# A two-layer hybrid decoder step: convolution, FFN, embedding and attention stages token-major, with the residual in HBM

## The reference

```python
for i in range(2):                                     # layer 0 convolution + FFN, layer 1 attention + experts
    hn = rms_norm(h, norm_mix[i])
    if i == 0:
        a, gate = split(hn @ w_pw1 + b_pw1)
        u = a * sigmoid(gate)
        u_ext = concat([past, u])                      # past: zeros, or 30 rows of state for sample tokens
        c = depthwise_conv(u_ext, w_dw) + b_dw         # 31 taps, causal
        y = silu(layer_norm(c)) @ w_pw2 + b_pw2
    else:
        q = head_rms_norm(hn @ w_q)                    # 16 heads
        y = softmax_window_sink(q, k, v) @ w_o         # keys t-128..t, one learned sink logit per head
    h = h + y
    hn = rms_norm(h, norm_ffn[i])
    h = h + (swiglu(hn) if i == 0 else top2_of_8_expert_swiglu(hn))
    h = h + sigmoid(rms_norm(h, norm_ple[i]) @ ple_gate[i]) * (p[i] @ ple_proj[i])
    if i == 0:
        s = rms_norm(h, norm_kv)
        k, v = head_rms_norm(s @ w_k), s @ w_v         # shared K/V; sample tokens add 128 cached rows
```

## Time and profile before

| | us |
|---|---|
| median of 3 runs (4354.18 to 4480.99) | 4356.48 |
| profiled run | 4348.89 |
| its span, slowest core (4335.1 to 4347.6 over the cores) | 4347.6 |

### The profile page before, as it was taken

How to read it: one execution, slowest core, us unless ns; L and a number is a source line. 1 busy time by engine, 2 the same in 40 slices (tenths; PEclk the granted TensorE clock), 3 DMA queues, 4 the chain that set the end, 5 groups by cost and what they waited for, 6 DMA issues and landing times.

```text
span 4347.6 us, 48773 instructions; the slowest of 8 cores (4335.1 to 4347.6 us)
## 1 busy us (share of the span) xinstructions
PE 2992.9 (69%) x20283; PEld 1866.0 (43%) x20291; DVE 1687.9 (39%) x2406; ACT 996.3 (23%) x1936; POOL 666.7 (15%) x728
## 2 busy tenths in 40 slices
PE   0365756656899968654664160269999999999654
PEld 0322222222455523211112020159987798888511
DVE  0132221224566674788995022631211122111154
ACT  0033233331111123343553000111111122111111
POOL 0010101000000004001502511211111111111144
PEclk9986877767999978878676575579999999999877
DMA  7500000003223120011501529359989899998254
GB/s 160 136 5 0 0 0 0 0 2 50 38 32 43 20 44 10 1 17 7 13 1 4 11 36 173 119 118 166 162 152 157 130 169 179 174 174 148 69 133 113
DMA packets 434769, 322.62 MB, mean 74 GB/s; under 512 B 312750, under 2 KB 356830, under 8 KB 434444
## 3 DMA queue, kind: packets, MB, share of 16 engines
q0 software_dynamic: 364416, 231.82, 35.7%
q1 hardware_dynamic: 64844, 76.85, 6.5%
q10 hardware_dynamic: 5280, 10.75, 1.0%
HBM read 475.67 MB, written 53.14 MB: 122 GB/s over the span
## 4 chain that ended last, share of the span: by engine, by line
PE 54%; DVE 14%; DMA 7%; issue 7%; ACT 5%; POOL 4%; DVEq 0%; POOLq 0%; ACTq 0%; SPq 0%
PE pb L1065 23%; PE pb L544 18%; PE pb L572 9%; DVE arena L1702 3%; DVE arena L1071 3%; DMA arena<-ck 3%; DVE arena L1083 2%; ACT arena L1225 1%; POOL arena L817 1%; DMA XG<-arena 1%; DMA arena<-arena 1%; POOL arena L171 1%; DVE arena L1705 1%; POOL XG L171 1%; POOL arena L159 1%
## 5 line engine op out<-in xcount | busy, mean ns | idle before, releaser
L1065 PE MATMUL pb<-arena 128*128 128x512 bf16 (+4 forms) x6284 | 1340.1, 376 | 463.2 <-ACT arena L1075 141.4
L1065 PEld LDWEIGHTS pb<-arena 128*128 128x128 bf16 (+1 forms) x6284 | 608.6, 104 | 1193.1 <-issue 288.5
L544 PE MATMUL pb<-arena 128*128 128x0 bf16 x7168 | 795.0, 274 | 0.8 <-DVE arena L505 0.8
L544 PEld LDWEIGHTS pb<-arena 128*128 128x128 bf16 x7168 | 679.1, 98 | 113.4 <-issue 1.1
L552 DVE TENSOR_TENSOR arena<-arena,pb 128x640 bf16<-128x640 f32 x224 | 184.0, 821 | 653.4 <-PE pb L544 647.7
L572 PE MATMUL pb<-arena 128*128 128x0 bf16 x3584 | 404.5, 274 | 0.0
L572 PEld LDWEIGHTS pb<-arena 128*128 128x128 bf16 x3584 | 337.7, 98 | 54.5
L551 ACT ACTIVATE arena<-pb 128x640 f32<-128x640 f32 x224 | 157.7, 704 | 617.2 <-PE pb L544 617.2
L1071 DVE RECIPROCAL arena<-arena 128x512 f32<-128x512 f32 (+2 forms) x92 | 245.9, 2673 | 76.6 <-ACT arena L1070 76.6
L1361 DVE TENSOR_TENSOR arena<-arena,pb 128x413 f32<-128x413 f32 (+1 forms) x440 | 225.8, 578 | 0.0
L1702 DVE RECIPROCAL arena<-arena 128x512 f32<-128x512 f32 x64 | 214.6, 3353 | 18.8 <-ACT arena L1698 17.3
(11 more groups left out here) (211 smaller groups left out, 2319.7 us busy)
## 6 DMA issues: line engine op xcount, KB each, us to landing
arena<-moe_gu POOLq DMA_DIRECT2D x224, 512.0 KB, 7.8
arena<-moe_d POOLq DMA_DIRECT2D x128, 448.0 KB, 9.2
XG<-arena ACTq DMA_DIRECT2D x1, 10240.0 KB, 69.5
arena<-XG SPq DMA_DIRECT2D x8, 1280.0 KB, 33.2
YD<-arena SPq DMA_DIRECT2D x8, 1280.0 KB, 18.3
arena<-x SPq DMA_DIRECT2D x16, 512.0 KB, 4.0
h4D<-arena SPq DMA_DIRECT2D x16, 512.0 KB, 2.8
arena<-h4D SPq DMA_DIRECT2D x16, 512.0 KB, 5.0
```

Of the source, the lines that this page charges most:

```text
L544: last = e.matmul(bank(b + h, HALF).shape_from_register(sr), w[:, a, kc, :], xg[:, kc, h * HALF:(h + 1) * HALF].shape_from_register(sr), s ...
L1065: last = e.matmul(banks[bk][0:prow, 0:ncols], l, rr, start=(i == 0), stop=(i == len(pairs) - 1))
```

## The change

Everything ahead of `Tail.experts` is written anew, token-major, the tokens of a tile on the partitions. The experts and the final stage keep their code. What it does, stage by stage:

- Weights are packed on the host in the order in which they lie in SBUF. The residual lives in HBM between the stages (h1D, h3D, h4D, fp32); x is loaded in 17 tiles where tile t holds the rows 16b+t. The norm of a tile is a Square with accumulated sum on ACT, an added eps on DVE, a power of -1/2 on POOL and one multiply on DVE, then eight transposes on PE.
- pw1 stays feature-major over tiles of 413 tokens (`T5`). Chunks 0 and 1 are issued inside the x loop. The copies to ks, vs and convs are queued on SP behind the x loop and in front of the past-row loads. u goes to HBM (uD, bf16) and comes back with 8 channels x 16 token phases on the partitions; the convolution of a chunk is then 48 matmuls of 128 columns against a tap matrix that DVE builds (`tbuild`, 6144 elements), adding b_dw on DVE out of PSUM, token-major.
- LayerNorm by bn_stats on DVE, one Identity pass and eight SiLU passes on ACT per pair of tiles; pw2 token-major; x is reloaded and b_pw2 added to it on POOL; the sum is stored to h1D.
- FFN: the activations `hact` of all 22 blocks stay in SBUF in bf16. The down product accumulates over 22 blocks in PSUM for each token tile, in one loop with the embedding term. The zero fill of XG is issued at block 4 of gate/up.
- K/V and Q weights are loaded as fp32 and scaled by the norm's gain on ACT and DVE, in memory that `hact` held until then.
- K/V, Q, attention, Wo and routing are one loop of 22 iterations, each working on up to five tiles in different steps. V has a column of ones, which gives the denominator; the mask is a multiply on DVE by 0 or 1; the reciprocal is of 128x16. The sample caches are loaded on the POOL queue in iterations 1 to 4 into one buffer and used in iterations 2 to 5. `route_b` is split in `route_l` and `route_c`. Nine units of the expert ring are loaded before the loop, the other 18 after it.

```diff
@@ x loop, and what follows it
+    for t in range(NB):
+        cur = xnorm(t)
+        if pend is not None:
+            xturn(*pend)
+        pend = cur
+        if nxt < NB:
+            pre_x(nxt)
+            nxt += 1
+        while oi < len(order) and T5[order[oi][1]][0] + T5[order[oi][1]][1] <= t * 128 and oi < 2 * (t - 3):
+            pw1(*order[oi])
+            oi += 1
+    S.dma("sp", ks[:, 0:127, :], ck[:, 1:128, :], "d2d0")
+    S.dma("sp", vs[:, 0:127, :], cv[:, 1:128, :], "d2d1")
+    S.dma("sp", convs[:, 0:29, :], sc[:, 1:30, :], "d2d2")
+    past_parts()
+    for c in range(8):
+        uout(c)
+        ustate(c)
+        if c >= 1:
+            conv(c - 1)
+        if c + 1 < 8:
+            tbuild(c + 1)
+        if c + 2 < 8:
+            for g in range(5):
+                pw1(c + 2, g)
+    conv(7)
@@ u round trip and convolution of a chunk
+    def uout(c):
+        S.dma("pool", uD[c * 128:(c + 1) * 128, :], u[:, 0:SEQ], "uo%d" % (c % 2), r=[u_r], w=[uD_r[c]])
+        S.dma("sp", U[:, :, 2:130], uD[c * 128:(c + 1) * 128, :].rearrange("(g c) (t b) -> (c t) g b", c=8, t=16), ...)
+    def conv(c):
+        for q in range(4):
+                for g4 in range(4):
+                    for dl in range(3):
+                        last = e.matmul(bank(bk, 128, 128, g4 * 128), U[:, g, 2 - dl:130 - dl], T[:, g, dl * 128:(dl + 1) * 128], ...)
+            S.op("dve", lambda e: e.tensor_tensor(out=ct[...], in0=bank(bk)[...], in1=bdw[...], op=ALU.add), ...)
@@ pw2
+    def x2_load(t):
+        S.dma("sp", b[0:n, :], xph[t] if t < 16 else xs[:, :], sem, w=[r_])
+        S.op("pool", lambda e: e.tensor_tensor(out=b[0:n, :], in0=b[0:n, :], in1=b2[0:n, :], op=ALU.add), r=[b2_r], w=[r_])
@@ FFN down
+                for h_ in range(2):
+                    for f in range(k0, k1):
+                        lt = hact[:, f, n_ * 128:n_ * 128 + n]
+                        last = e.matmul(bank(bk + h_, 512, n), lt, Wd[:, f, h_ * 512:(h_ + 1) * 512], start=(f == 0), stop=(f == NF - 1))
@@ sample caches
+    def s_load(sg):
+        for si in range(4):
+            S.dma("pool", KA5[0:127, si, :, 0, :], ck[s_, 1:128, :]..., "ka%d" % si, w=[KA_r], part=(si > 0))
+            S.dma("pool", VA5[0:127, si, :, 0, :], cv[s_, 1:128, :]..., "va%d" % si, w=[VA_r], part=(si > 0))
+            S.dma("pool", V05[0:1, si, :, 0, :], cv[s_, 0:1, :]..., "v0%d" % si, w=[V0g_r], part=(si > 0))
@@ the attention loop
+    for i in range(17 + 5):
+        if on is not None:
+            ot = o_turn(*on)
+        if qk is not None:
+            qk_turn(*qk)
+        if i == 1:
+            s_load(0)
+        xt_ = x_turn(*xn_) if xn_ is not None else None
+        for g in range(4):
+            if na is not None:
+                scores(na, g)
+            if g == 0 and xt_ is not None:
+                lo_ = tl.route_l(*xt_, 6, 256)
+            if g == 1 and lo_ is not None:
+                tl.route_c(*lo_, 6, 256)
+            if np_ is not None:
+                pv(np_, g)
+            if g == 1 and ot is not None:
+                xn_ = oproj(*ot)
+        if np_ is not None:
+            on = onorm(np_)
+        if nq is not None:
+            qk = qkv(nq)
+        if 2 <= i < 6:
+            s_att(i - 2)
+            if i < 5:
+                s_load(i - 1)
+    tl.ring_open(PRE, tl.RING_N)
```

More of the change, by code:

```diff
@@ new lines, in s4_out @@
+    def s4_out(n_, n, xn, xn_r):
+        bk = nb()
+        turn(xn, xn_r, n, bk)
+        xT, xT_r = xT4.next()
+        copy("act", xT[:, :, 0:n], turned(bk, n), [b_r[bk]], [xT_r])
+        S.dma("sp", x3D[n_ * 128:(n_ + 1) * 128, :].rearrange("p (k c) -> p k c", k=8)[:, :, 0:n], xT[:, :, 0:n], "x3s%d" % ((n_ + 1) % 17 % 4), r=[xT_r], w=[x3D_r[n_]])
+    S.dma("sp", gp0, rows[7:8, :].to_broadcast([128, D]), "gp0", w=[gp0_r])
+    for i in range(2):
+        s4_load(order4[i])
+    q1 = q2 = None
@@ new lines, in build, with scores, fn @@
+    pgs = {}
+    def scores(n_, g):
+        qT, qT_r, kT, kT_r, _, _ = kvs[n_]
+        bs = pair()
+        k0 = 0 if n_ > 0 else 1
+        kt = {1: (kT, kT_r)}
+        if n_ > 0:
+            kt[0] = kvs[n_ - 1][2:4]
+        def fn(e):
+            last = None
+            for kb in range(k0, 2):
+                for hf in range(2):
+                    sl = slice(64 * hf, 64 * hf + 64)
+                    last = e.matmul(bank(bs + hf, 256, 128, kb * 256), kt[kb][0][sl, g, :], qT[sl, 2 * g:2 * g + 2, :], start=True, stop=True)
+            return last
+        S.op("pe", fn, r=[qT_r] + [v[1] for v in kt.values()], w=[b_r[bs], b_r[bs + 1]])
+        pb, pb_r = Pr.next()
+        src = P[:, bs * 512:(bs + 2) * 512].rearrange("p (h c) -> p h c", h=2)[:, :, k0 * 256:512]
+        dst = pb[:, :, k0 * 256:512]
+        S.op("act", lambda e: e.activation(out=dst, in_=src, func=AF.Exp), r=[b_r[bs], b_r[bs + 1]], w=[pb_r])
+        mk = maskt.rearrange("p k j q -> p (k j q)")[:, k0 * 256:512].unsqueeze(1).to_broadcast([128, 2, 512 - k0 * 256])
+        S.op("dve", lambda e: e.tensor_tensor(out=dst, in0=dst, in1=mk, op=ALU.mult), r=[c_mask], w=[pb_r])
+        pgs[(n_, g)] = (pb, pb_r)
@@ new lines, in o_turn, with oproj, fn @@
+    def o_turn(n_, ob, ob_r):
+        turn(ob, ob_r, 128, 6)
+        OT, OT_r = OTr.next()
+        copy("dve", OT, turned(6, 128), [b_r[6]], [OT_r])
+        return n_, OT, OT_r
+    def oproj(n_, OT, OT_r):
+        n = rowsof(n_)
+        bo = pair()
+        def fn(e):
+            last = None
+            for h in range(2):
+                for kc in range(8):
+                    last = e.matmul(bank(bo + h, 512, n), OT[:, kc, 0:n], Wo[:, kc, h * 512:(h + 1) * 512], start=(kc == 0), stop=(kc == 7))
+            return last
+        S.op("pe", fn, r=[OT_r, Wo_r], w=[b_r[bo], b_r[bo + 1]])
+        h, h_r = h5t.pop(n_)
+        S.op("dve", lambda e: e.tensor_tensor(out=h[0:n, :], in0=P[0:n, bo * 512:(bo + 2) * 512], in1=h[0:n, :], op=ALU.add),
+             r=[b_r[bo], b_r[bo + 1]], w=[h_r])
+        S.dma("sp", h4D[n_ * 128:n_ * 128 + n, :], h[0:n, :], "h4s%d" % (n_ % 4), r=[h_r], w=[tl.h4D_r[n_]])
+        ms, rs, ms_r, rs_r, _ = mcol(n)
+        xn, xn_r = xn5.next()
+        square(h[0:n, :], xn[0:n, :], ms, n, [h_r], ms_r, xn_r)
+        powh(ms, rs, ms_r, rs_r, n)
+        S.op("dve", lambda e: e.scalar_tensor_tensor(out=xn[0:n, :], in0=h[0:n, :], scalar=rs, in1=gf1[0:n, :], op0=ALU.mult, op1=ALU.mult),
+             r=[h_r, rs_r, gf1_r], w=[xn_r])
+        return n_, n, xn, xn_r
@@ L1732, in build, with s_first2, s_att @@
+    def s_first2():
+        turn(K0s, K0s_r, NS, 4, nk=4)
+        copy("dve", k0T, turned(4, NS, 4), [b_r[4]], [k0T_r])
+    def s_att(sg):
+        b0 = pair()
         for hb in range(2):
-            bk = nb()
             def fnt(e):
@@ L1795, in build @@
[L1795 to L1799 removed]
+                    e.matmul(bank(b2_, 4, 128, col), VA[:, si, g * 128:(g + 1) * 128], PA[:, col:col + 4], start=True, stop=False)
```

1795 lines of the change are left out of this document (838 added, 957 removed).

## The result

The changed kernel takes 3571.09 us (median of 4 runs, 3564.76 to 3643.28) against 4370.66 us of the kernel before on the same chip: ratio 0.8176 with a 95% interval of 0.8119 to 0.8233. Its profiled execution spans 3562.8 us; the prediction's sum was 3322 us, forecast 3325, range 3020 to 3515. The direction was right, the sum was short by 241 us, and the time lies above the upper end of the range. Some executions ran with one die at a lower granted clock; the ratios leave them out, where a run has no ratio its profiled execution stands for it, and f4_two_buffers is read on a core of the other die.

What follows compares the result with a forecast made beforehand. The prediction took the chain between engines to bound all changeable stages but the PE-full FFN. Its terms A to G summed to 3322 us; a few us more for the median gave the forecast 3325 us, range 3020 to 3515.

Steps and rivals of the forecast that it cites:

- F: K/V/Q, attention, Wo and routing in one loop: 661 us, loaded iterations 62 us each, full ones 27.5 us.
- C: LayerNorm, pw2 and norm: 222 us, 24 us a pair of tiles, with POOL's x reload and bias add in the chain.
- E: Wkv/Wq staging after the last down matmul: 50 us with PE idle, 42 us of it for 8 MB.
- D: FFN: gate/up 315 us, down with the embedding term 258 us, the zero fill lying beside gate/up.
- A: Load, norm, pw1 of two chunks and past rows: 158 us, all on the path.
- B: Convolution loop: 145 us, six chunks with pw1 at 20 us each, plus 25 us for the last two.
- G: Transition to the experts 36 us, as ring units compete with gathered rows; experts and final stay at 1477 us.
- R3: Rival, expert ring starvation: gain lost only from 6.6 us a unit, then 4350 us or more; chance 0.04.
- R2: Rival, the clock falls in stages with gaps and DVE and POOL ports collide: 3519 us; chance 0.19.

Runs made afterwards that it cites:

- f4_two_buffers: The changed kernel with a second set of sample cache buffers, so a group loads while the one before is used; ratio 0.8154.
- g1: The changed kernel with the nine expert units issued in iteration 7 of the attention loop instead of beside the K/V and Q weights; span 3525.6 us.
- f1: The changed kernel loading only the first of four cache groups, the other samples reading the same data; 3415.35 us, ratio 0.7849.
- g3: The changed kernel with expert units 11 to 26 waiting for the first gathered rows to land before they are issued; span 3540.0 us.

## Why the prediction fell short

The steps that failed are four terms of the sum: the period of a loaded iteration in F (62 us, measured 79 to 88), the copy that C left out, the bytes that E left out, and the fill and drain that D left out.

- **A, B.** Right in size; in A two errors cancel. The first past-row multiply came at 127.8 us instead of about 105, the HBM-to-HBM copies having been issued at 72.5 us instead of 61 and the last of them having landed at 115; and the four rounds took 36 us instead of 53 (127.8 to 164). B's chunks were 18.6 us apart. The tap matrix was priced right, 6.55 us.
- **C.** The failed step is the chain of a pair, "22 to 26 us", and the engines' work of a tile in front of it: DVE's copy back into natural order has no term there, so it was put at nothing without a reason ("eight transposes and a copy" stands in A alone). The kernel writes it with a step of 16 elements. It took 4.46 us, where the same shape contiguous takes 0.69; taking it off DVE gives 45 of the 67 us. The mechanism named instead, POOL's reload and add, is half true: 20 us, with the add at 2.35 us. The earlier trace rows had no strided write at all, so the step needed a bound from both sides, and got none.
- **D.** Matmul prices held: the sixteen full tiles took 15.5 us each against 15.2. Gate/up lost 15.4 us at one place: the zero fill, which the prediction let lie "beside gate/up". It is issued on ACT's queue, and the small second transfer behind the large one held ACT:

```profile
691.60 229.00 PE L1358 MATMUL pb<-arena 128*128 128x412 bf16 x1296 [15.39 <-ACT arena L1364]
...
664.15 26.75 ACTq L149 DMA_DIRECT2D YD<-arena  x1
691.03 0.92 ACT L1364 ACTIVATE arena<-pb 128x413 f32<-128x413 f32 x2 [26.81 <-issue]
```

The first line is PE's, waiting for ACT's pass over the PSUM banks, the others are ACT's. Of a step that is moved, its DMAs must be followed on the queue that it goes to; I did not ask who else lives on ACT's. The rest of D is fill and drain: the first, 16-token tile took 23 us and the steps behind the last down matmul 26, neither in a sum of 17 x 15.2. All of D I read from the trace; no run varied it.
- **E.** 50 against 71: the failed step is the 42 us for 8 MB, without the units' bytes on the same DMA engines. g1 gave back 26 to 29 us, so without the units the term would have come out at 42 to 45.
- **F.** The 97 us are 72 in the first and loaded iterations (365 against 293), 6 in the free ones (308 against 302) and 19 in the five draining ones (85 against 66), which I had only guessed and no run varied. The failed step is the period of the loaded ones, 62: 38.6 us of issue was right, and so in size were 10 for landing and 10 for the buffer (10 and 8.3), but the sum left out the gaps between the transfers of one queue and the iteration's own 14 us, which do not lie beside the load but behind it, since the head norm's pow and the loads share POOL. So 79 to 88 instead of 62; f1 took 47 us off each.
- **G.** Transition 40 against 36, with the named cause confirmed by g3 (11 us less); experts unchanged, no starvation, so R3's condition never came near: 343 units arrived within 1222 us.
- **R2** (3519 us, chance 0.19) was nearest in size, for a reason that the runs don't bear out: the granted clock was 0.75 in the free iterations, and they still took 27.8 us. Port waits are not visible as a lump either: the mask multiplies on DVE kept 0.69 us.

The range failed for a reason of its own. Its upper end took in a lower clock and port waits, but no pricing error in a chain of waits; four such errors of 21 to 97 us, all upward, went past it.

On the mask: L1228 of the earlier trace rows is no all-bf16 case, as I had written; its second operand, the taps, is fp32 in the code. With both operands bf16 the multiply took 0.688 us for 1024 elements a partition. By the Trainium skill ("VectorE: DVE Perf Modes", section "The perf-mode tier table") such a multiply runs at twice the rate, which makes about 0.6 us, an estimate; the 0.688 us of the runs is near it.
